# Gate columns of the input projection: tokens as the moving operand, on four column quarters of TensorE

## The reference, cut to what matters

```python
proj = (h @ w_in).astype(f32)
conv_in, z_a, a_a, b_a, q_b, k_b, v_b, o_b, i_b, f_b = _split(proj, SPLITS)
g_a = -jnp.exp(gdn_a_log.astype(f32)) * jax.nn.softplus(a_a + gdn_dt_bias.astype(f32))
beta_a = jax.nn.sigmoid(b_a)
```

## Time and profile before

| | |
|---|---|
| median of three runs | 1353.22 us (1351.71 to 1355.7) |
| the profiled execution | 1356.39 us, of which the span of its instructions is 1354.6 us |
| TensorE busy | 1303.1 us, 96% of the span |
| VectorE, ScalarE, GpSimd busy | 533.4, 206.6 and 46.9 us |
| mean granted TensorE clock | 0.984 |
| gate columns on TensorE (L564) | 48 records, 21.6 to 30.4 us |

### The profile page before, as it was taken

One profiled execution on the slowest core, in us unless ns is written; L12 is line 12 of the kernel. 1 busy time (PEld: TensorE's weight loads), 2 busy tenths in 40 slices (PEclk: granted clock), 3 DMA queues, 4 the chain that ended last, 5 costly groups with the idle time before them and its releaser, 6 DMA issues.

```text
span 1354.6 us, 17116 instructions
## 1 busy us (share of the span) xinstructions
PE 1303.1 (96%) x6312; PEld 565.7 (42%) x6312; DVE 533.4 (39%) x1157; ACT 206.6 (15%) x408; POOL 46.9 (3%) x100
## 2 busy tenths in 40 slices
PE   6999999889999999999999999999999999999997
PEld 5765687544433333333333333333333333333332
DVE  2484345854363243323343332333332333333223
ACT  2351111041111110011110110100110100011112
POOL 5100001100000000000000000000000000000000
PEclk9999999989799999999999999999999999999999
DMA  8232110135699999999999999999999999999931
GB/s 259 80 124 67 62 60 7 70 131 169 212 370 429 428 428 428 429 429 428 428 430 428 428 429 428 430 428 430 428 429 429 428 429 428 429 428 429 429 150 39
DMA packets 56373, 438.30 MB, mean 324 GB/s; under 512 B 12570, under 2 KB 19879, under 8 KB 31738
## 3 DMA queue, kind: packets, MB, share of 16 engines
q1 hardware_dynamic: 56346, 437.93, 78.1%
HBM read 432.89 MB, written 5.02 MB: 323 GB/s over the span
## 4 chain that ended last, share of the span: by engine, by line
PE 75%; DMA 16%; DVE 5%; issue 2%; ACT 1%; SPq 1%; POOL 0%; POOLq 0%; ACTq 0%; DVEq 0%
PE bank L1077 26%; DMA ring<-in_expert_w_gu 16%; PE bank L1088 12%; PE bank L582 8%; PE bank L1033 4%; PE bank L1063 4%; PE bank L1182 2%; PE bank L1098 2%; PE bank L752 2%; PE bank L580 2%; PE bank L1041 1%; PE bank L1010 1%; PE bank L661 1%; PE bank L673 1%; PE bank L1066 1%
## 5 line engine op out<-in xcount | busy, mean ns | idle before, releaser
L1077 PE MATMUL bank<-ring,SC 128*64 128x512 f32 x2048 | 474.0, 599 | 4.3 <-DVE SC L1996 1.0
L1077 PEld LDWEIGHTS bank<-ring,SC 128*64 128x64 f32 x2048 | 136.2, 136 | 290.0 <-issue 257.1
L1088 PE MATMUL bank<-ring,SC 128*64 128x512 f32 x1024 | 226.8, 595 | 0.0
L2026 DVE TENSOR_TENSOR SC<-bank,bgu 128x256 f32<-128x256 f32 x128 | 48.2, 418 | 224.9 <-PE bank L1098 224.9
L1088 PEld LDWEIGHTS bank<-ring,SC 128*64 128x64 f32 x1024 | 70.6, 137 | 133.3 <-issue 127.6
L582 PE MATMUL bank<-xT,ring 128*128 128x320 f32 x384 | 113.9, 445 | 4.7 <-ACTq L1274 3.7
L1996 DVE TENSOR_TENSOR SC<-bank,gmoe 128x512 f32<-128x512 f32 x33 | 22.8, 692 | 219.1 <-PE bank L1041 219.1
L2013 DVE TENSOR_TENSOR X<-X,bank 128x512 f32<-128x512 f32 x120 | 76.9, 682 | 49.8 <-PE bank L1063 49.8
L1033 PE MATMUL bank<-XS,SC 128*64 128x512 f32 x396 | 90.6, 592 | 0.7 <-issue 0.7
L1389 ACT ACTIVATE SC<-bank 128x512 f32<-128x512 f32 x33 | 19.7, 598 | 452.6 <-PE bank L1033 452.6
L2017 DVE TENSOR_TENSOR X<-X,bank 64x256 f32<-64x256 f32 x120 | 50.1, 418 | 92.2 <-PE bank L1066 90.4
(11 more groups left out here) (456 smaller groups left out, 1068.2 us busy)
## 6 DMA issues: line engine op xcount, KB each, us to landing
ring<-in_expert_w_gu SPq DMA_DIRECT2D x128, 2048.0 KB, 20.1
ring<-in_expert_w_down SPq DMA_DIRECT2D x64, 2048.0 KB, 21.0
ring<-in_w_in SPq DMA_DIRECT2D x7, 2048.0 KB, 8.5
ring<-in_w_out SPq DMA_DIRECT2D x2, 2048.0 KB, 8.4
ring<-in_ple_gate_w SPq DMA_DIRECT2D x4, 1024.0 KB, 14.5
out_gdn_s<-ring SPq DMA_DIRECT2D x1, 2048.0 KB, 10.6
X<-in_x_prompt SPq DMA_DIRECT2D x2, 512.0 KB, 4.2
SC<-in_ple_w SPq DMA_DIRECT2D x1, 1024.0 KB, 5.2
```

Of the source, the lines that this page charges most:

```text
L1077: last = mm(PB[j][SL * h:SL * h + SL, :], xg[:, c % 4, c // 4, :], w[:, FF * h + 512 * j:FF * h + 512 * j + 512], start=(c == 0), stop=(c ...
L1088: last = mm(PB[4][SL * h:SL * h + SL, :], act_t[:, 2 * (c - NGU) + kk, :], w[:, D * kk + 512 * h:D * kk + 512 * h + 512], start=(c == NGU ...
L2026: ins = V.tensor_tensor(out[:, 4 * i:4 * i + 4, :], PB[2 + i][:, :].rearrange("p (k h s) -> p k h s", k=4, h=2)[:, :, h, :], bgu[:, c0 + 4 ...
```

## The change

The 16 gate columns become the stationary operand, padded with zeros to 32 columns, and all 320 tokens move. Slice k = 4i + g goes to column quarter g, that is to partitions 32g to 32g+31 of bank 0, so that each quarter holds the sum over two of the eight slices, with the gate columns on the partitions and the tokens along the row. VectorE copies this 128x320 block to `SC`. After one more projected chunk (`fill(KD)`) three matmuls with the tokens of the copy as the stationary operand and 16 columns of `stack` as the moving one sum the four quarters and turn the result, so that it lies where it lay before. `stack` is four identities of 32x32 above each other, which VectorE makes from `ident` at the start. The projected chunks behind it are regrouped: one before the new matmuls, two before the running sums and three after them, where there were two and four. GpSimd fills the padding.

```diff
-        w16 = sb("w16", [P, KD, 16])
+        w16 = sb("w16", [P, KD, 32])
+        stack = sb("stack", [P, 32])
@@ gpsimd
             fill(g16[:], 0.0)
+            fill(w16[:, :, 16:32], 0.0)
             fill(gcb[:], 0.0)
@@ tensor
             pe.wait_ge(sem("pcol"), 1)
-            for t in range(3):
-                R = ROWS[t]
-                for k in range(KD):
-                    last = mm(PB[0][0:R, 16 * t:16 * t + 16], xT[:, k, OFF[t]:OFF[t] + R], w16[:, k, :],
-                              start=(k == 0), stop=(k == KD - 1))
+            pe.wait_ge(sem("consts"), CONSTS["consts1"])
+            for i in range(2):
+                for g in range(4):
+                    last = mm(PB[0][32 * g:32 * g + 32, 0:NTOK], w16[:, 4 * i + g, :], xT[:, 4 * i + g, :], start=(i == 0), stop=(i == 1),
+                              skip_group_check=True)
             last.then_inc(sem("g16_ps"), 1)
@@ tensor
+            fill(KD)
+            pe.wait_ge(sem("g16_part"), 1)
+            pe.wait_ge(sem("stack"), 1)
+            for t in range(3):
+                last = mm(PB[0][0:ROWS[t], 16 * t:16 * t + 16], SC[:, 6, OFF[t]:OFF[t] + ROWS[t]], stack[:, 0:16], start=True, stop=True)
+            last.then_inc(sem("g16_ps"), 1)
             fill(2 * KD)
             pe.wait_ge(sem("gl8"), 1)
@@ tensor
-            fill(4 * KD)
+            fill(3 * KD)
             norm_pair(0)
@@ vector
+            dve.wait_ge(sem("consts"), CONSTS["consts0"])
+            tell(V.tensor_reduce(stack[:, :], ident[:, :].rearrange("p (g e) -> p e g", g=4), AX, ALU.add), "stack")
             norm()
@@ vector
             dve.wait_ge(sem("g16_ps"), 1)
+            tell(V.tensor_copy(SC[:, 6, 0:NTOK], PB[0][:, 0:NTOK]), "g16_part")
+            dve.wait_ge(sem("g16_ps"), 2)
             dve.wait_ge(sem("small_in"), 96)
             V.tensor_copy(g16[:, 0:2, :].rearrange("p t g -> p (t g)"), PB[0][:, 0:32])
```

## The result

The changed kernel takes 1344.29 us (median), the kernel before 1353.22 us: ratio 0.9937, 95% interval 0.9915 to 0.9959, so 8.5 us less, between 5.5 and 11.5. The forecast was 1346.2, 7.0 less. Two more measurements of the same kernel gave 0.9918 (0.9903 to 0.9932) and 0.9951 (0.9934 to 0.9968). All are faster by more than 0.3%. One of the nine executions of the changed kernel took 1690 us at a granted clock of 0.747, where the others have 0.98, and is left out of the ratio. The profiled execution took 1344.29 us with a span of 1342.5, 12.1 less than the profiled one of before. That is more than the medians differ by, and much of what follows is about why.

A forecast was written before the change was run, and what follows sets the result against it. TensorE's unbroken chain bounds the start, a full DMA stream the expert loop's end, which moves with it. -8.83 + 1.2 + 0.6 = -7.0 us from the median 1353.22 gives 1346.2 us; own range 1344 to 1348.5, eight in ten 1343.0 to 1349.8.

The forecast's parts named there:

- Removed: Gate columns at the start: 48 thin TensorE records fully on the path go away, saving 8.83 us.
- The quarters: Eight gate matmuls, 16 records of 320 columns, four running together: 1.2 us added at the high rate.
- The sum: Three matmuls, six records, that sum the four quarters: 0.6 us added.
- rival (2): Quarter matmuls with 320 columns run one after another: 4.3 us instead of 1.2, time 1349.3; 5%.
- (1): Weight loads of the quarters not hidden: 1.7 to 2.8 us added, time 1347.9 to 1349.0; 4%.
- The low-rate stretch: TensorE's slow start of wide work: again 4.9 us, now from 21.62 over quarters and some projection, loss the same.
- Rival (3): Quarters don't raise TensorE's rate: they cost 2.2 us, projection keeps its slow stretch; saving 6.0, time 1347.2; 14%.
- The late VectorE list: VectorE waits for the summed gates before gate arithmetic and convolutions: lag about 3.6 us, gone after two convolutions.
- rival (4): VectorE's later gate arithmetic and convolutions stay in the path: saving only 3.4 us, time 1349.8; 8%.
- the DMA stream moves with what is in front of it: Expert loop: a full DMA stream sets its end but starts after TensorE and VectorE work, so earlier gains pass through.
- (5): No change: something fixed in time further on, or the timing of low-rate stretches, takes the gain back; 6%.
- rival (6): Slower by over 4.1 us: an earlier start places clock pauses behind the recurrences, 250 to 375 us, differently; 4%.

The follow-up runs named there:

- e5: Changed kernel with all eight gate matmuls in one column quarter (partitions 0 to 31), copy and sum using these alone; 1348.42 us, ratio 0.9977 to the kernel before.
- e1: The changed kernel measured again, no edit; 1343.19 us, ratio 0.9918 to the kernel before.
- e11: Second run of the changed kernel with eight extra 512-column matmuls at the start, into an unused bank; 1344.28 us, ratio 0.9935.
- e2: The kernel before measured again, no edit; ratio 0.9993 against itself.
- e9: Changed kernel with three projected chunks in front of the sum instead of one; 1345.57 us, ratio 0.9958.
- e10: The changed kernel measured a third time, no edit; 1344.11 us, ratio 0.9951.
- e6: Changed kernel with the eight quarter matmuls done four times over, adding 48 records; ratio 0.9973.
- e4: The kernel before with eight extra 512-column matmuls at the start, into an unused bank; ratio 0.9991.
- e7: The kernel before with one projected chunk in front of the thin gate records and three, not four, behind the running sums; ratio 0.9983.
- e8: Changed kernel with no projected chunk between quarters and sum, four behind the running sums; 1347.18 us, ratio 0.997.

## Why the prediction was right

**The work removed and added.** Removed 8.83 us, as in every profile of the kernel before. The quarters were costed at 1.2 at the high rate and 2.2 at the low one and take 1.28 and 2.36. The sum was put at 0.6 and takes 0.57. The quarters do overlap with 320 moving columns: 80 ns a record at the high rate, against 110 ns for the load of each, and against 5.81 us for the same 16 records in one quarter (e5), which is what rival (2) would have looked like. Rivals (1) and (2) are out.

**The low-rate stretch** is the term that was mis-sized. The working kept it equal in both kernels, 4.9 us from the first wide work, and had it end at 26.5 us in the changed one. In e1 and e11, which start slow, it ends near 24.8, 3.2 and 3.8 us after the quarters begin; in e2 at about 35, 4 us after the projection begins. Comparing two executions that both start slow, e2 and e1, the parts are: gates -6.47, sum +0.57, the six chunks -1.44 (10.90 + 17.42 against 4.95 + 8.81 + 13.12), in all 7.4 us where 7.0 was said. So the projection behind the quarters loses 1.4 us less than it did behind the thin records. And in three profiles with nothing added at the start (the first, e9, e10) the rate had risen before the quarters began, which wins another 1.5 us. Why the rate rises at one point in one execution and at another in the next was not found. Rival (3), that quarters don't bring the rate up, is refuted by e6.

**What the change is worth without the luck.** With a slow start 7.4 us from e2 to e1, 7.8 from the first profile to e1, 6.8 from e4 to e11. For a fast start there is no profile of the kernel before; e7, which has one part of the change in it but the same gate records met at the high rate, needs 35.77 us where the changed kernel needs 29.76, so 6.0 us stand in for it. The 9.8 us between the first two profiles pair a slow start of before with a fast one of after. The forecast of 7.0 lies inside 6.0 to 7.8, for nearly the right reasons: removed, added and covered work came as costed, and the stretch that was mis-sized makes 0.9 to 1.9 us between these three pairs.

**The late VectorE list.** The lag of 3.6 us was to be gone after two convolutions, and the third was put at 41; it starts at 38.52 in a faster execution, 9.8 us before its old time, as TensorE. e9 adds 8.6 us to that lag and still shows no wait and no later `norm_pair`, which refutes rival (4).

**The passage to the end.** From the start of the expert loop every one of the 13 profiles takes 962.4 to 963.9 us. That is what "the DMA stream moves with what is in front of it" meant, and it holds. Rivals (5) and (6) placed the danger between `norm_pair` and the loop. There the profiles need 323.6 to 332.5 us, and the mean granted clock from 250 to 375 us goes with it: 0.84 to 0.85 for those of 328.6 us or more, 0.86 to 0.89 for those below 326. The three profiles of the changed kernel are 328.93, 330.94 and 323.63, those of the kernel before 330.33 and 330.68: this decides up to 7 us between two executions of one kernel, as much as the effect itself. The prediction set rival (6) aside because three runs of the kernel before lay within 4 us of each other; its nine executions go from 1347.21 to 1355.94, and those of the changed kernel, without the one of 1690 us, from 1339.82 to 1349.05. The scatter was thus taken too small, even though the rival didn't come true.

**What stays open.** The medians say 8.5, 11.1 and 6.6 us, the stage by itself 6.0 to 7.8. The interval of the second, 9.2 to 13.1 us, leaves out the forecast and doesn't meet that of the third, 4.3 to 8.9; so the measurements differ by more than their own intervals allow, and that the first came within 1.5 us of the forecast is in part luck. Whether the rest is chance in where the later slow stretches fall, or whether the earlier start makes them shorter on average, these few profiles can't tell. It wasn't tried, either, what would keep the rate up from 250 to 375 us. No version tried was better than the changed kernel beyond the intervals.

## What to carry to other kernels

A float32 matmul that moves few columns over a wide stationary operand pays for loading the operand (in e7, for 16 moving columns and at the high rate, 0.11 us a record with 128 stationary columns and 0.06 with 64): swap the two, pad the narrow side to 32 columns, spread the contraction over the four column quarters, and sum the quarters with one small matmul against stacked identities. Count what stands next to such thin work as well: here it ran at half rate, and even where it began at the full rate (e7) it handed half rate on to the wide matmuls behind it. Before believing a difference of a few microseconds between two profiles, look at the same stage in a second profile of each.

## What was not expected of the hardware

Thin records cost more than their own time: met at the high rate (e7) the first 32 took 0.11 us each, but the granted clock fell to 0.50 before all 48 were through, and 16 projected matmuls behind them took 2.7 us longer. The transposes in front stood on the edge: with the same instructions the last four took 0.48 us in some executions and 0.70 in others, and in e4 the rate fell in the middle of them, though eight wide matmuls had run just before. How long after the start of the quarters the rate rose differed between 3.2 us (e1), 5.7 (e6) and 7 (e8). In e8, with a pause of 0.57 us and six thin records in that time, these records and the two chunks behind them took 2.1 us longer than at the full rate; that the pause and the records caused it isn't shown. In profiles whose first recorded change of the clock comes late, the granted clock reads 1.00 where the spacing of the records shows half rate; the spacing is the thing to read there.
